# Second pass of the input projection: context's pair first, channels before z in each turn

## The reference, cut to what matters

```python
h = rmsnorm(x, norm_pre_mix[l]) * (1.0 + sc1) + sh1
hc = rmsnorm(ctx, norm_pre_mix[l]) * (1.0 + sc1c) + sh1c
...
q, k, v, g, z, xbc, dtf, dtb = split_proj(h @ w_in)
qc, kc, vc, gc, zc, xbcc, dtfc, dtbc = split_proj(hc @ w_in)
...
u = jax.nn.silu(short_conv(xbc, conv_w, conv_b))
```

## Time and profile before

| | us |
|---|---|
| median of 3 runs | 2426.53 (2424.98 to 2428.33) |
| the profiled execution | 2426.86 |
| its span in the trace | 2425.2 |
| TensorE busy in the span | 2209.7 (91%) |
| VectorE, ScalarE, GpSimd busy | 1399.5, 1056.5, 645.2 |
| mean granted TensorE clock | 0.959 |

### The profile page before, as it was taken

How to read it: one execution, slowest core, us unless ns; L and a number is a source line. 1 busy time by engine, 2 the same in 40 slices (tenths; PEclk the granted TensorE clock), 3 DMA queues, 4 the chain that set the end, 5 groups by cost and what they waited for, 6 DMA issues and landing times. The chain is left out here.

```text
span 2425.2 us, 35328 instructions
## 1 busy us (share of the span) xinstructions
PE 2209.7 (91%) x11572; PEld 1835.8 (76%) x11573; DVE 1399.5 (58%) x2063; ACT 1056.5 (44%) x1517; POOL 645.2 (27%) x646
## 2 busy tenths in 40 slices
PE   7999999999997769997999839999999999999890
PEld 4788888899997658886888737777777777777770
DVE  3422222376555658886577745855666664647776
ACT  3332232243223136665222225745666664546763
POOL 0000000000000648886122232222333333223213
PEclk9999999999998979998999869999999999999995
DMA  8542333656553976664553245987988887758997
GB/s 280 191 157 97 125 122 155 180 160 199 167 176 98 368 272 220 224 221 171 182 192 139 105 143 149 350 277 217 309 257 257 277 250 229 230 165 256 349 349 293
DMA packets 302556, 518.78 MB, mean 214 GB/s; under 512 B 38486, under 2 KB 211062, under 8 KB 297704
## 3 DMA queue, kind: packets, MB, share of 16 engines
q1 hardware_dynamic: 276040, 439.52, 53.5%
q0 software_dynamic: 17216, 44.60, 8.4%
q10 hardware_dynamic: 9216, 33.56, 3.4%
HBM read 397.28 MB, written 129.09 MB: 217 GB/s over the span
## 5 line engine op out<-in xcount | busy, mean ns | idle before, releaser
L2385 DVE TENSOR_TENSOR e_w_low<-e_w_whole,e_w_high 128x2048 fp32r<-128x2048 f32 x192 | 431.2, 2288 | 92.3 <-ACT e_w_high L2337 91.2
L2337 ACT ACTIVATE e_w_high<-e_w_whole 128x2048 fp32r<-128x2048 f32 x192 | 356.4, 1907 | 24.6 <-PEq L1680 12.0
L2291 PE MATMUL e_pG<-e_w_high,e_xT 128*128 128x512 f32 x768 | 305.2, 397 | 1.2 <-ACT e_xT L2330 1.2
L2292 PE MATMUL e_pG<-e_w_low,e_xT 128*128 128x512 f32 x768 | 305.1, 397 | 0.0
L810 PE MATMUL proj_acc<-w_high,hT_high 128*128 128x512 f32 x672 | 264.3, 393 | 3.8 <-DVE hT_low L892 3.8
L810 PE MATMUL proj_acc<-w_low,hT_high 128*128 128x512 f32 x672 | 262.7, 391 | 0.0
L810 PE MATMUL proj_acc<-w_high,hT_low 128*128 128x512 f32 x672 | 262.6, 391 | 0.0
L2310 PE MATMUL e_pY<-e_w_high,e_hT 128*128 128x512 f32 x768 | 224.7, 404 | 0.0
L2295 PE MATMUL e_pG<-e_w_high,e_xT 128*128 128x512 f32 x768 | 195.6, 397 | 0.0
L1076 DVE SCALAR_TENSOR_TENSOR conv_out<-ch,cw,conv_out 128x258 f32<-128x258 f32 x288 | 120.4, 482 | 94.4 <-ACT conv_out L721 94.2
L2291 PEld LDWEIGHTS e_pG<-e_w_high,e_xT 128*128 128x128 f32 x768 | 145.2, 189 | 37.0 <-issue 1.6
(11 more groups left out here) (290 smaller groups left out, 4160.8 us busy)
## 6 DMA issues: line engine op xcount, KB each, us to landing
e_w_whole<-in_moe_w_gate_dram SPq DMA_DIRECT2D x64, 1024.0 KB, 8.2
e_w_whole<-in_moe_w_up_dram SPq DMA_DIRECT2D x64, 1024.0 KB, 11.0
e_w_whole<-in_moe_w_down_dram SPq DMA_DIRECT2D x64, 1024.0 KB
by_token<-tok SPq DMA_DIRECT2D x32, 512.0 KB, 3.6
w_in_raw<-in_w_mod_dram SPq DMA_DIRECT2D x32, 512.0 KB, 3.7
m_tok<-by_token SPq DMA_DIRECT2D x16, 768.0 KB, 5.5
s_kv<-by_token SPq DMA_DIRECT2D x20, 512.0 KB, 5.7
modulated_high<-hT_high SPq DMA_DIRECT2D x9, 1024.0 KB, 3.9
```

Of the source, the lines that this page charges most:

```text
L2291: nc.tensor.matmul(pG[:, half], xT[:, 0, k], wh[:, half, w], start=(k == 0), stop=False)
L2292: nc.tensor.matmul(pG[:, half], xT[:, 0, k], wl[:, half, w], start=False, stop=False)
L2337: nc.scalar.activation(wh[:, third, part], raw[:, third, part], ACT.Copy).then_inc(whs.sem, 1)
L2385: nc.vector.tensor_tensor(wl[:, third, part], raw[:, third, part], wh[:, third, part].bitcast(F32), ALU.subtract).then_inc(wls.sem, 1)
```

## The change

Context's pair comes first in the second pass (turn t works on pair t), and the outputs of a turn are ch0, ch0, ch1, ch1, z, z in banks 0 to 5. The weights follow: ch0 takes the place of q, ch1 that of k, z that of v, loaded in this order. ScalarE has the first silu of z behind silu 2 and the second behind silu 3, which now stands in the same turn. SyncE stores the z of a turn at the start of the next, ahead of the slabs, and all four block pairs of a turn within it. The two z stores of the last turn are the last transfers of the stage. `mod_sum`, the dt turn and the sums keep their places behind outputs 3 and 1, which are channels now.

```diff
-    PLACE = {"q": 0, "k": 1, "v": 2, "g": 3, "z": 0, "ch0": 1, "ch1": 2}
+    PLACE = {"q": 0, "k": 1, "v": 2, "g": 3, "ch0": 0, "ch1": 1, "z": 2}
     OUTS = ([(c, j) for c in "qkvg" for j in range(2)] + [("dt", 0)],
-            [(c, j) for c in ("z", "ch0", "ch1") for j in range(2)])
+            [(c, j) for c in ("ch0", "ch1", "z") for j in range(2)])
+    Z = 4
...
-    SPLIT = ("dt", "g", "z", "ch0", "ch1")
-    FREED = {"z": 1, "ch0": 3, "ch1": 5}
+    SPLIT = ("dt", "g", "ch0", "ch1", "z")
+    FREED = {"ch0": 1, "ch1": 3, "z": 5}
...
     def is_ctx(p, t):
-        return t == (LAST_TURN if p else 0)
-
-    def pair_of(p, t):
-        return t if p == 0 else (t + 1) % NGR
+        return t == 0
...
                 else:
-                    is_ready(sp, 1, u - 2, 5)
+                    is_ready(sp, 1, u - 2, made(1, u - 2)[-1])
...
-                    sp.dma_start(h[:, s].rearrange("p k t -> p (k t)").bitcast(F32), dram[name][pair_of(1, u)]).then_inc(h_in.sem(s), 16)
+                    sp.dma_start(h[:, s].rearrange("p k t -> p (k t)").bitcast(F32), dram[name][u]).then_inc(h_in.sem(s), 16)
...
-                if u:
-                    store_u(u - 1, 3)
-                load_slab(4 * u + 2)
-                if not is_ctx(1, u):
-                    store_z(u)
-                load_slab(4 * u + 3)
-                store_u(u, 0)
-                load_slab(4 * u + 4)
-                store_u(u, 1)
-                load_slab(4 * u + 5)
-                store_u(u, 2)
+                if u and not is_ctx(1, u - 1):
+                    store_z(u - 1)
+                for b in range(4):
+                    load_slab(4 * u + 2 + b)
+                    store_u(u, b)
...
-            store_u(LAST_TURN, 3)
+            store_z(LAST_TURN)
...
             def take(t, b):
 
-                o = b + 2
+                o = b
...
+            def gate(t, j):
+                is_ready(act, 1, t, Z + j)
+                if t > 1:
+                    act.wait_ge(z_out.sem(j), z_out.at(t - 2))
+                nc.scalar.activation(zt[:, j], acc[:, Z + j], ACT.Silu).then_inc(eact[1].sem, 1)
+
             for t in range(NGR):
-                if not is_ctx(1, t):
-                    for j in range(2):
-                        is_ready(act, 1, t, j)
-                        if t:
-                            act.wait_ge(z_out.sem(j), z_out.at(t - 1))
-                        nc.scalar.activation(zt[:, j], acc[:, j], ACT.Silu).then_inc(eact[1].sem, 1)
-                if t:
-                    silus(t - 1, 3)
...
                     take(t, b)
                     if b:
                         silus(t, b - 1)
-            silus(LAST_TURN, 3)
+                if is_ctx(1, t):
+                    silus(t, 3)
+                else:
+                    gate(t, 0)
+                    silus(t, 3)
+                    gate(t, 1)
```

More of the change, by code:

```diff
@@ L391, in u_column @@
         def u_column(t, b_width):
-            return (CONTEXT_AT if is_ctx(1, t) else LATENT_AT + pair_of(1, t) * 2 * P) - 2, b_width
+            return (CONTEXT_AT if is_ctx(1, t) else LATENT_AT + t * 2 * P) - 2, b_width
         @block.sync
@@ L499, in _ @@
             load_h(0)
-            for n in pieces_of("z"):
+            for n in pieces_of("ch0"):
                 load_w(n)
             store_qk(LAST_TURN)
-            for c in ("ch0", "ch1"):
+            for c in ("ch1", "z"):
                 for n in pieces_of(c):
@@ L542, in store_u @@
                 sp.wait_ge(silu.sem, silu.at(t, b + 1))
-                c0, width = u_column(t, OUT if t >= LAST_TURN - 1 else 2 * P)
+                c0, width = u_column(t, OUT if t in (0, LAST_TURN) else 2 * P)
                 sp.dma_start(dram["u"][2 * b:2 * b + 2, :, c0:c0 + width].rearrange("c p t -> p c t"), v[:, 2 * b:2 * b + 2, 0:width]).then_inc(u_out.sem(b), 16)
@@ L547, in store_z @@
                 for j in range(2):
-                    left(sp, 1, t, j)
-                    sp.dma_start(dram["tok"][pair_of(1, t) * 2 + j, :, 4 * 512:5 * 512], zt[:, j]).then_inc(z_out.sem(j), 16)
+                    left(sp, 1, t, Z + j)
+                    sp.dma_start(dram["tok"][t * 2 + j, :, 4 * 512:5 * 512], zt[:, j]).then_inc(z_out.sem(j), 16)
             def load_rows(n):
@@ L685, in _ @@
                         high(n)
-            z, ch0, ch1 = (pieces_of(c) for c in FREED)
-            for n in z:
+            first, second, third = (pieces_of(c) for c in FREED)
+            for n in first:
                 high(n)
             evacuate(LAST_TURN, 4)
-            for n in ch0:
+            for n in second:
                 high(n)
@@ L694, in _ @@
             evacuate(LAST_TURN, 6)
-            for n in ch1[:2]:
+            for n in third[:2]:
                 high(n)
@@ L698, in _ @@
             evacuate(LAST_TURN, 8)
-            for n in ch1[2:]:
+            for n in third[2:]:
                 high(n)
@@ L974, in _ @@
                         low(n)
-            z, ch0, ch1 = (pieces_of(c) for c in FREED)
+            first, second, third = (pieces_of(c) for c in FREED)
             turned(LAST_TURN, 0)
             turned(LAST_TURN, 1)
-            for n in z[:2]:
+            for n in first[:2]:
                 low(n)
             turned(LAST_TURN, 2)
-            for n in z[2:]:
+            for n in first[2:]:
                 low(n)
             turned(LAST_TURN, 3)
-            for n in ch0 + ch1:
+            for n in second + third:
                 low(n)
@@ L1079, in taps @@
                     to = chb[:, 2 * b:2 * b + 2, 0:4]
-                    if t == LAST_TURN - 1:
+                    if is_ctx(1, t):
                         m = V.memset(to, 0.0)
```

## The result

| | before | after |
|---|---|---|
| median of 14 runs each, same chip | 2427.18 (2424.51 to 2430.82) | 2432.01 (2429.97 to 2437.75) |
| ratio, 95% interval | | 1.0019 [1.0012, 1.0027] |
| profiled execution, its span | 2426.86, 2425.2 | 2432.09, 2430.5 |
| first product of the second pass | 461.37 | 459.88 |
| TensorE's last slot of the stage ends | 771.37 | 780.92 |

The change costs 4.8 us where 5.9 was forecast: a real slowdown, since the interval leaves 1 out, just at the 0.2% that this measurement can tell. The page's first line and its busy times, to be read beside the earlier trace rows: the same work in a longer span.

A forecast was written before the change was run, and what follows sets the result against it. TensorE was taken to bound the second pass. It ends 9.8 us later, plus 0.5 for rows, minus 4.7 at the end, plus 0.3 for stores: 5.9 us slower, 2432.4 us; range 2427.5 to 2437.0.

The forecast's parts named there:

- Part 1: TensorE's second pass: the same products in another order, nothing added or removed, 10.91 us of z moved; alone worth nothing.
- Part 2: Turn 1 begins in banks not yet free: TensorE waits 6.69 us, then 3.45, and ends 9.8 us later.
- The pin: Turn 1's third product is held to 513.16 by VectorE's chain, through bank 2's copy, whatever happens ahead of it.
- the cover: The 3.45 us wait before bank 2 takes in the first wait's low clock, 1.7 to 3.2 us, costed at nothing.
- Part 3: Load of turn 2's rows, queued on SyncE behind turn 0's last channel store: 0 to 1.7 us, taken as 0.5.
- Part 4: Stage's end, z now last: 3.63 us instead of 8.33, 4.7 gained, less 0.3 for three stores close together.
- What follows: Later stages: the same instructions behind a barrier, shifting with the stage's end, no change in them.
- Rival A: Turn 1's banks come free earlier because small loads land sooner; up to 10.14 us less, 2421.5; chance 0.06.
- Rival B: Next stage gives some back after TensorE's shorter idle: up to 3.2 us of low clock saved, 2429.2; chance 0.16.
- Rival C: Clock stays low through turn 1's first two products, third product 9.4 us past 513.16: 2441.8; chance 0.08.

The follow-up runs named there:

- e5: The change with ScalarE's four copies of turn 0's channels moved ahead of the step sizes' chain: 2432.37 us against 2426.46 before, ratio 1.0028.
- e8: e7 with the running sums' product put behind output 2 of turn 1 instead of output 1: 2422.45 us against 2426.11 before, ratio 0.9986.
- e10: e8 with the four early copies put back where the change has them: 2433.13 us against 2427.06 before, ratio 1.003.
- e1: The kernel before with only context's pair first, z still ahead of the channels: 2433.83 us against 2426.11 before, ratio 1.0028.
- e6: e5 with turn 2's rows loaded ahead of all of turn 0's stores: 2428.81 us against 2426.46 before, ratio 1.0007.
- e7: e6 with ScalarE's exponentials put behind the first two copies of turn 1: 2423.74 us against 2426.46 before, ratio 0.9988.
- e9: e1 with turn 2's rows loaded right after the slab of turn 1 is issued: 2429.22 us against 2426.11 before, ratio 1.0018.
- e3: The change with the 17 small loads issued by GpSimd instead of SyncE: 2429.30 us against 2426.11 before, ratio 1.0005.
- e4: The kernel before with the 17 small loads issued by GpSimd instead of SyncE: 2433.85 us against 2426.11 before, ratio 1.0031.

## Why the prediction was right, and where it was off

The place, the cause and the sign of each step were right. The forecast was 1.1 us too high by the medians. That the time itself, 2432.4, is met to 0.4 us is in part luck, since before's median rose from 2426.53 to 2427.18 with more runs. At the stage's end it had 785.56 (781.13 + 0.5 + 3.93), and the row stands at 784.29, 1.27 less. By its steps:

- **Part 1.** The forecast starts the pass at 461.37, as in the trace of before; in the trace of after it began 1.49 us earlier, and that and 0.5 us more was lost by the end of turn 0: 0.4 waiting for the rows of the dt turn, 1.0 in the dt turn, 0.6 to more low clock behind it. It changes nothing, because the banks hold turn 1 anyway. Slots as read: from turn 2's start to the last slot's end 245.68 us, worked out 245.54. The dt turn was not the 4.12 taken from before but 5.13, since the clock fell within it and not behind it; turn 0 ended at about 490.6, not 490.12.
- **Part 2.** Forecast: 6.69 us of wait to 496.81, then a wait before the third product, pinned to 513.16. Measured: 5.7 from slot to slot (5.59 in the row) to 496.34, then to 512.66. ScalarE's copies came 0.55 earlier than in the trace of before, with SyncE's small loads (their first issue at 472.23 against 472.90). The pin held: without clock cost the third product would have been wanted at 496.34 + 11.52 + 1.38 = 509.24, 3.42 us ahead of 512.66. The sums' turn began at 510.45 instead of 507.86, so the low clock cost 2.59 us of these 3.42. The forecast had 1.7 to 3.2 for it and booked it at nothing, rightly. Only 0.8 us of the cover were left, though; more low clock than that would have shown.
- **Part 3.** 0.5 was taken for turn 2's rows, 0.05 us of wait is there. The half that took 9.4 us before took 8.3.
- **Part 4.** The end was to shrink by 4.7 - 0.3 = 4.4; it shrank from 8.33 to 3.37, by 4.96. The 0.3 for stores in a burst were not there: the last z store went out at 781.74 and GpSimd began 2.55 us later, against 2.81 for the last store of channels. The last turn's channels were through 1.4 us before the end, forecast 1.0. That store landed in 2.0 us. The Trainium skill (DMA: Bandwidth & Descriptors, Anatomy of one DMA) has a fixed 2.0 us or so plus the bytes at peak rate for a transfer that GpSimd issues, which is 2.6 us, as an estimate, for one of this size. This one was issued by SyncE, so the figure doesn't hold for it, and the measurement decides.
- **What follows.** From GpSimd's row to the span's end it is 1645.5 before and 1646.2 after, as forecast, but a single execution does not carry this far: on the way the two traces drift by more than that. The lag is 4.6 us where `states` begins, 3.35 where `mixing` does, and 1.6 at the first product of `residual`. GpSimd's and TensorE's rows of before, then of after:

```profile
862.23 0.52 POOL L1413 MEMSET m_zero<- 128x512 f32 x1 [2.97 <-POOLq L1119]
...
1387.17 1.97 PE L1899 MATMUL r_pT<-ident,r_h 128*128 128x128 f32 x8 [6.33 <-DVE r_h L2043]
```

```profile
865.58 0.52 POOL L1408 MEMSET m_zero<- 128x512 f32 x1 [2.98 <-POOLq L1114]
...
1388.80 1.97 PE L1894 MATMUL r_pT<-ident,r_h 128*128 128x128 f32 x8 [6.33 <-DVE r_h L2038]
```

`states` alone took between 80.4 and 84.0 us in the twelve traces, with the same instructions. That the later stages neither give back nor take rests on the medians, which follow the stage's end in the table above.

Sum of the misses: turn 2 starts 0.85 earlier than forecast (0.40 of it the copies and the work behind them, 0.45 the rows), the turns behind it are 0.14 longer, and the end is 0.56 shorter: 0.85 - 0.14 + 0.56 = 1.27.

**Rival A** (banks free earlier): the chain came 0.55 us forward, not the 5.7 that it needs to turn faster. As a mechanism it is right: once the copies are forward by another way (e5 to e8), the change becomes faster, though only after the other waits on the same late chain have been cleared. The prediction gave 10.14 us as its price, and e10 against e8 has 9.3 to 10.6; its 2421.5 for a run without these waits stands beside e8's 2422.45. What it missed is that this price is not paid back by the copies alone: the sums' turn, the rows and turn 1's exponentials had come within 2 to 4 us of TensorE unseen, hidden by the first wait.
**Rival B** (the next stage gives some back): its mechanism is there, its gain can't be shown. After a wait of 8.4 us instead of 13.5 TensorE works at the low level for 2.7 us (789.49 to about 792.2), before for 6.0 (784.99 to about 791.0). `states` is 1.2 us shorter in this pair of traces, which is inside its spread of 3.6, and the median did not come down by it: +4.8 us stands beside the +4.6 with which the stage began.
**Rival C** (clock low through two products) fell: it was full again by about 502.3. The Trainium skill (TensorE: Matmul & The Clock Gate, Loop structure matters more than you think) has a long wait between products followed by the lower clock. Behind 5.6 us here, behind 3.5 and 3.3 in e1, and behind 3.9, 3.6, 2.3 and 2.0 in e5 and e6, the traces agree; behind 1.81 in e7, 2.57 in e10 and 3.09 in e9 they show the full one.

## What to carry to other kernels

When work moves to the end of a turn to shorten a tail, ask what now stands first, in whose banks, and which engine's first-turn chores (small loads, a long setup chain) hold the copy that frees them; before the move the order itself was the cover. A stall that is removed uncovers the next one on the same late chain: list for each consumer of the chain when it is wanted and when it comes, and move all of them, or the gain stays at nothing (e5) until the last is done (e7, e8). And measure a gain apart from its price by giving both versions the same obstacle (e3 against e4): here some 4.6 us of gain were there all along.

## What was not expected of the hardware

- With the small loads issued by GpSimd, at least nine of the seventeen (1 to 256 KB) were in flight beside the 32 KB store of the steps, which took 6.2 us (e3) and 6.4 (e4) to land instead of 3.5, and TensorE waited 4.4 and 4.6 us for its rows, where it was 0.3. Whether the queue, the small packets or the one load of 256 KB does it was not told apart.
- A short wait of TensorE can cost more than itself: behind 3.3 us in e1 the next two outputs took 1.7 us longer. But a longer wait does not always bring the lower clock where a shorter one does: the granted clock over the next 6 to 6.5 us was 0.74 behind 2.03 us in e6 and behind 3.53 in e1, and 1.00 behind 2.57 in e10 and 3.09 in e9. What tells them apart stays open.
- The same dt turn took 4.19 us before, 5.20 after and 7.73 in e3, with the same instructions; only the clock's fall moved, from behind it into it, and in e3 ahead of it.
